# Moving the 8-byte tile of the scaled epsilon behind the weight tiles, in a two-block transformer kernel on one core

## What is computed

```python
def swiglu(h, w_gate, w_up, w_down):
    return (jax.nn.silu(h @ w_gate) * (h @ w_up)) @ w_down

for l in range(2):                                   # first block
    x = x + 0.5 * swiglu(rms_norm(x, ffn1_norm[l]), ...)
    h = rms_norm(x, mix_norm[l])
    a, g, q, k, v = split(h @ w_in[l])               # causal conv of 31 taps; differential attention
    q, k = rms_norm(q, q_norm[l]), rms_norm(k, k_norm[l])
    x = x + concat(conv_out, diff_out) @ w_out[l]
    x = x + 0.5 * swiglu(rms_norm(x, ffn2_norm[l]), ...)
for l in range(2):                                   # second block
    mod = silu(c) @ ada_w[l] + ada_b[l]
    x = x + g1 * (retention_mixer, sgu_mixer)[l](modulate(rmsnorm(x, ...), ...))
    x = x + g2 * peer_ffn(modulate(rmsnorm(x, ...), ...), w_query, sub_keys, expert_u, expert_v)
return rmsnorm(x, norm_final)
```

## The kernel before

| tile | address before | modulo 64 | address after | modulo 64 |
|---|---|---|---|---|
| x, h_hi, h_lo, sq, tmp_h | 4224 to 33919 | 0 | the same | 0 |
| ident, ones | 33920, 34432 | 0 | the same | 0 |
| qeps (8 bytes, takes 32) | 38976 | 0 | 96960 | 0 |
| mod, gs, lam | 39008, 39392, 39520 | 32 | 38976, 39360, 39488 | 0 |
| subg | 39616 | 0 | 39584 | 32 |
| raw (3 x 8192) | 39648 | 32 | 39616 | 0 |
| w_hi (4 x 4096) | 64224 | 32 | 64192 | 0 |
| w_lo (4 x 4096) | 80608 | 32 | 80576 | 0 |
| arena | 97408 | 0 | the same | 0 |

## Time and profile before

### The profile page before, as it was taken

One profiled execution on the slowest core, in us unless ns is written; L12 is line 12 of the kernel. 1 busy time (PEld: TensorE's weight loads), 2 busy tenths in 40 slices (PEclk: granted clock), 3 DMA queues, 4 the chain that ended last, 5 costly groups with the idle time before them and its releaser, 6 DMA issues.

```text
span 3235.5 us, 53578 instructions
## 1 busy us (share of the span) xinstructions
PE 3125.6 (97%) x22724; PEld 2921.9 (90%) x22724; DVE 2217.6 (69%) x3454; ACT 1623.5 (50%) x2442; POOL 187.5 (6%) x153
## 2 busy tenths in 40 slices
PE   8999999999999999999899999999989999999999
PEld 7998999999899889999899998878989988999887
DVE  5767776776687645799655556665659985555665
ACT  5644544655554345455444444456445554444444
POOL 0000000000000000730000000000037000000000
PEclk9999999999999999999999999999999999999999
DMA  6663476775277444446766656645444577666663
GB/s 222 242 235 105 171 251 237 256 258 182 77 257 254 169 161 152 156 170 248 266 216 209 214 202 232 210 164 194 157 149 177 205 257 242 209 215 213 210 232 117
DMA packets 153262, 654.63 MB, mean 202 GB/s; under 512 B 10332, under 2 KB 77472, under 8 KB 78272
## 3 DMA queue, kind: packets, MB, share of 16 engines
q1 hardware_dynamic: 96576, 584.09, 50.9%
q10 hardware_dynamic: 56032, 65.66, 6.3%
q0 software_dynamic: 416, 1.45, 0.2%
HBM read 616.55 MB, written 34.61 MB: 201 GB/s over the span
## 4 chain that ended last, share of the span: by engine, by line
PE 73%; DVE 19%; ACT 5%; DMA 2%; issue 1%; POOL 1%; ACTq 0%; DVEq 0%
PE ps L583 15%; PE ps L585 14%; PE ps L584 14%; PE ps L588 8%; PE ps L589 8%; PE ps L590 8%; DVE w_lo L1502 5%; DVE at L2007 2%; DVE at L2002 2%; ACT w_hi L1069 2%; PE ps L739 1%; DVE at L2005 1%; DVE raw L1497 1%; POOL w_lo L2079 1%; DVE at L1926 1%
## 5 line engine op out<-in xcount | busy, mean ns | idle before, releaser
L1502 DVE TENSOR_TENSOR w_lo<-raw,w_hi 128x1024 fp32r<-128x1024 f32 x932 | 1134.8, 1224 | 694.3 <-ACT w_hi L1069 693.4
L1069 ACT ACTIVATE w_hi<-raw 128x1024 fp32r<-128x1024 f32 x1000 | 1051.2, 1055 | 754.6 <-PE ps L585 460.9
L583 PE MATMUL ps<-h_hi,w_hi 128*128 128x256 f32 x4224 | 1194.9, 283 | 19.2 <-DVE w_lo L1502 14.2
L585 PE MATMUL ps<-h_hi,w_lo 128*128 128x256 f32 x4224 | 1185.3, 281 | 0.0
L584 PE MATMUL ps<-h_lo,w_hi 128*128 128x256 f32 x4224 | 1185.3, 281 | 0.0
L583 PEld LDWEIGHTS ps<-h_hi,w_hi 128*128 128x128 f32 x4224 | 796.8, 189 | 27.2 <-issue 15.1
L584 PEld LDWEIGHTS ps<-h_lo,w_hi 128*128 128x128 f32 x4224 | 796.5, 189 | 3.3 <-issue 0.2
L585 PEld LDWEIGHTS ps<-h_hi,w_lo 128*128 128x128 f32 x4224 | 796.3, 189 | 0.0
L588 PE MATMUL ps<-w_hi,at 128*128 128x512 f32 x1024 | 406.8, 397 | 11.7 <-DVE at L2025 11.7
L589 PE MATMUL ps<-w_lo,at 128*128 128x512 f32 x1024 | 406.5, 397 | 0.0
L590 PE MATMUL ps<-w_hi,at 128*128 128x512 f32 x1024 | 406.2, 397 | 0.0
(11 more groups left out here) (274 smaller groups left out, 3149.3 us busy)
## 6 DMA issues: line engine op xcount, KB each, us to landing
raw<-in_peer_u SPq DMA_DIRECT2D x128, 1024.0 KB, 4.8
raw<-in_peer_v SPq DMA_DIRECT2D x128, 1024.0 KB, 4.8
raw<-in_ffn_gu SPq DMA_DIRECT2D x88, 1024.0 KB, 5.0
raw<-in_ada_w SPq DMA_DIRECT2D x48, 1024.0 KB, 5.1
raw<-in_ffn_down SPq DMA_DIRECT2D x44, 1024.0 KB, 5.1
gates<-at ACTq DMA_DIRECT2D x32, 1024.0 KB, 5.2
at<-gates ACTq DMA_DIRECT2D x24, 1024.0 KB, 6.0
raw<-in_w_in SPq DMA_DIRECT2D x16, 1024.0 KB, 4.9
```

Of the source, the lines that this page charges most:

```text
L583: e.matmul(o, lhs[0], rhs[0], start=start, stop=False)
L585: return e.matmul(o, lhs[1], rhs[0], start=False, stop=stop)
L1069: e.activation(whi[:, u % NPAIR, :], raw(k, half), ACT.Copy).then_inc(hi_done.hit(u), 1)
L1502: e.tensor_tensor(wlo[:, m % NPAIR, :], raw(k, half), whi[:, m % NPAIR, :].bitcast(FP), ALU.subtract).then_inc(w_lo_dve.hit(m), 1)
```

## The change

One allocation moves from behind `rcol` to behind `w_lo`. The instructions, their order and their waits are the same on all engines. `qeps` gets a new address, and the tiles between its old place and its new one lie 32 bytes lower, as in the table above.

```diff
@@ -187,7 +187,6 @@
         epsc = sb("epsc", [128, 2])
         rr = sb("rr", [128, T])
         rcol = sb("rcol", [128, 2])
-        qeps = sb("qeps", [128, 2])
         mod = sb("mod", [128, L, 48])
         gs = sb("gs", [128, L, 16])
         lam = sb("lam", [128, 20])
@@ -195,6 +194,7 @@
         raw_t = sb("raw", [128, NRAW, 2 * UNIT])
         whi = sb("w_hi", [128, NPAIR, UNIT], FR)
         wlo = sb("w_lo", [128, NPAIR, UNIT], FR)
+        qeps = sb("qeps", [128, 2])
```

## The result

| | before | after |
|---|---|---|
| time, median | 3234.78 us (3233.81 to 3236.18, 4 runs) | 3194.39 us (3188.39 to 3202.14, 4 runs) |
| the profiled execution | 3237.27 us, span 3235.5 us | 3191.61 us, span 3189.8 us |
| granted TensorE clock, mean | 0.991 | 0.987 |

The ratio of the times, after to before, is 0.9876, with a 95% interval from 0.9853 to 0.99: 40 us less.

A forecast was written before the change was run, and what follows sets the result against it. The prediction took the kernel to be bound by the rate at which PE puts one matmul behind the other. Every term was taken as 0 us, so the median stayed at 3234.3 us, range 3219 to 3256 us.

The forecast's parts named there:

- What bounds the kernel: Whole kernel: PE, busy 97% of the span, is bound by the rate at which one matmul follows the other.
- the three values: Distances between starts of 256-column matmuls before the change: 117.3, 118.7 or 120.0 ns, with no cause in other engines or DMAs.
- qeps, DVE, ACT: The qeps writes and reads, DVE's splits and ACT's roundings at new addresses: 0 us, at most 0.2 us either way.
- POOL: POOL's part of the splits in the expert layers: 0 us, bounded by 4.8 us of gain or loss.
- DMA: Loads of 1 MB into raw: 0 us, to 0.1 us for each load, hidden by three buffers.
- PE at half rate: Float32 matmuls at half rate: the 32-byte offset costs PE nothing in either role, 109 ns each at both offsets.
- PE at the full rate: fp32r matmuls reading weights: excess over the columns taken as independent of address, 0 us; bounds 210 us less, 30 us more.
- The first rival: PE's two read streams, both at 0 modulo 64, settle in the fastest value, 117.3 ns: 3219 to 3228 us, chance 0.22.
- The bound from the half-rate matmuls: Weight matmuls at 109 and 218 ns if the half piece caused the excess: 210 us less, 3024 us, chance 0.05.
- The slowest rival: Both PE streams want their next 64-byte piece at once, matmuls go towards 120.0 ns: 3241 to 3264 us, chance 0.23.
- The reshuffle: Long PE stretches fall into other values without direction, some 4 us, within 0.2%; counted with no change, together 0.50.
- What would show it: Profile after: same distances 117.3, 118.7, 120.0, 233.5 ns, split 1224, rounding 1055, PE's waits at same lines within 2 us.

The follow-up runs named there:

- e3: The changed kernel with activations and arena also moved up 32 bytes, so every tile PE reads stands at 32 modulo 64: 3192.85 us, ratio 0.9866.
- m1: Only TensorE matmuls, computation left out, weights at ten places 0 to 256 bytes behind h: 113.3 to 120.0 ns at 256 columns, 226.7 to 237.3 at 512.
- m2: The sweep: TensorE alone, one weight tile stepped by 8 bytes from 0 to 504 against h, then 512, 576, 1088: 113.3 to 122.0 ns at 256 columns.

## Why the prediction was wrong, point by point

*What bounds the kernel* was right: the distance between PE's starts. (Its own counts give 117.4 and 120.2 ns where it says 117.3 and 120.0; the starts give the latter.) It was also right that the three values belong to PE itself and not to other engines or DMAs; the kernels with TensorE alone show the same values.

*qeps, DVE, ACT* at 0 us were right. The split stays at 1224 ns and the rounding at 1055 ns, and with `raw` alone moved the ratio is 1.0003. *POOL* at 0 with a bound of 4.8 us: PE's waits for it are 5.4 us, 0.6 more. *DMA* at 0: 4.8 us for 1 MB in both, and the kernel with `raw` alone at 192 modulo 256 shows nothing within 0.2%. The 0.4% of a load that the Trainium skill (DMA: Bandwidth & Descriptors, How a descriptor splits into AXI transactions) lets estimate is too small to be told apart here. *PE at half rate* at 0: its tiles are `ident`, `ones` and the arena, which the change leaves where they were, so the result doesn't test it.

***PE at the full rate: "I take 0"*** is the step that failed. It measured -63 us in the profiled execution, of which 17 us were given back in waits and lower clock, where the sum had nothing for either. The term's bounds, -210 and +30 us, held it; the stated range didn't. Three steps of the reasoning were wrong, as the runs show:

1. "It grows nearly with the columns that pass, whichever of the two tiles stands at 32 ... That speaks for a cost of reading float32 at this rate, whatever the address." The two rows compared (256 and 512 columns) both had their tiles 96 bytes apart. They changed the roles and not the quantity that counts, and so could not show that it doesn't count. There was a contrast in the trace, between those rows and the expert layers at a difference of 32, but 32 and 96 happen to give the same 233.3 ns, and I hadn't seen that they were two differences at all.
2. "One of which is always a `w` tile (32 modulo 64) and the other one always a tile at 0 modulo 64." True, but modulo 64 is the wrong measure. It made all stretches look alike, and made "both at 0" the case to think about. By e3 both may stand at 32, and by m1 and m2 the period is 256.
3. The first rival had the mechanism right: "a pattern that depends on where they start against each other; 32 bytes are 8 columns of one against the other". It was given 0.22 and a floor of 3219 us, since I took 117.3 ns, the best value already seen, as the best that there is. A new difference brings a new set of values (113.3 and 117.8), not a choice among the old ones. The bound from the half-rate matmuls, 3024 us, should have stood at that rival too.

*The slowest rival* (fetches of 64 bytes at the same moment) had its sign wrong for this change. But slower places exist: 0 and 24 bytes are 0.4 and 0.5% slower than before. That nothing can be said of the sign from the trace of before alone was a fair reading of it; that the size is small was not.

*The reshuffle* exists as scatter: each stretch of the kernel after takes 113.3 or 117.8 ns anew at each start, and its nine runs lie within 18 us (3187.2 to 3205.6). The kernel before had 1.4 ns between its two usual values, and of its 45 runs beside the experiments 44 lie within 10 us (3230.4 to 3240.5; one took 3249.3).

*What would show it* was the useful part: "I am wrong if a value appears that isn't among the three, ... or if the distance at 512 columns leaves 233.5 ns". Both happened. PE's waits stayed at the same lines, but those for DVE's splits grew by 2.9 us, where it had said within 2.

What stays open is why. No run here shows what the two streams share. The Trainium skill (SBUF — State Buffer, SBUF: two separate sides) says that only the port pair shared by GpSimd and VectorE causes contention and that PE never waits on anyone. For other engines the runs agree: m1 has the kernel's values with all of them idle. But the place of PE's own two operands costs a matmul of 256 columns up to 17 ns more than its columns (123.3 - 106.7). Which of the two reads is held up, no run separates. Also open is why whole kernels show values that the sweep didn't (at 24, and 120.0 ns at 76). What picks the value at an entry is open too, but it isn't chance alone: at a difference of 64, both moved by a multiple of 32 bytes, the entry after two tiny matmuls took 117.8 ns in ten of ten and the one after three took 113.3 ns in nine of ten. The loss by lower clock and waits was read from the traces, not tested.

## What to carry to other kernels

Where TensorE is busy nearly all the time with float32 at full rate, look at the distance between matmul starts, and try the place of the weight tiles against the activation tiles as a setting of its own: a few bytes of padding are worth from +0.5% to -1.7% here. A kernel with matmuls alone ranks the places in one run; the whole kernel must then say how much of it is left. And when rows are alike under two conditions, ask whether the quantity in question differs between them before it is called without effect, and don't take the best value seen as the best possible.

## What the hardware showed that I had not expected

- A matmul of 256 columns of fp32r takes from 113.3 to 123.3 ns from start to start at full clock, one of 512 columns from 226.7 to 240.0 ns, with nothing changed but the addresses of its two operands.
- The values repeat every 256 bytes of difference (at all 32 places tried), and every 32 bytes when both tiles move together (with two entries that don't fit).
- At one pair of addresses PE can have two or three values. It takes one when it starts again, and keeps it for as long as it isn't interrupted: it changed in none of the 144 uninterrupted stretches of over 60 matmuls before and after, the longest of 1139. With TensorE alone it is half and half at a difference of 64, and always the same one at 8 (115.6) and at 76 (113.3). In the whole kernel 8 keeps its one value, and 76 shows 120.0 as well.
- The two roles don't agree on the best difference: 0 is the best one at 512 columns (226.7 ns) and a bad one at 256 (120.0 ns).
